# One load with a repeated source for the base blocks, and the evacuations of transposed keys and values on ScalarE

## What is computed

```python
k_beta = k * beta[..., None]
v_beta = v * beta[..., None]
L = jnp.where(strict, jnp.einsum('bhncd,bhnmd->bhncm', k_beta, k) * decay, 0.0)
T_mat = lax.linalg.triangular_solve(eye + L, jnp.broadcast_to(eye, L.shape),
                                    left_side=True, lower=True, unit_diagonal=True)
u = jnp.einsum('bhncm,bhnmd->bhncd', T_mat, v_beta)
w = jnp.einsum('bhncm,bhnmd->bhncd', T_mat, k_beta * jnp.exp(g)[..., None])
k_to_end = k * jnp.exp(g_last[..., None] - g)[..., None]
```

## Time and profile before

| | us |
|---|---|
| median of 3 runs | 1362.94 (1361.47 to 1365.14) |
| profiled execution, whole | 1355.06 |
| its span, first to last instruction | 1353.3 |
| PE busy | 1294.6 (96%) |
| PE weight loads busy | 1088.4 (80%) |
| DVE busy | 940.7 (70%) |
| ACT busy | 708.2 (52%) |
| POOL busy | 228.8 (17%) |
| mean granted PE clock | 0.977 of full speed |

### The profile page before, as it was taken

The page is one execution under the profiler, slowest core; times in us unless marked ns, Lnnn a source line. Parts: engine busy times, 40 slices in busy tenths (PEclk is TensorE's granted clock), DMA queues, the critical chain, the costliest instruction groups (busy, mean ns, idle before and its releaser), DMA issues.

```text
span 1353.3 us, 20838 instructions
## 1 busy us (share of the span) xinstructions
PE 1294.6 (96%) x6906; PEld 1088.4 (80%) x6906; DVE 940.7 (70%) x1703; ACT 708.2 (52%) x1288; POOL 228.8 (17%) x293
## 2 busy tenths in 40 slices
PE   5999979999999979989999999999999999999996
PEld 4676769857888757878888888888888888888885
DVE  5697696646765535566978888888788885555554
ACT  5454444424434664546566656665666555444442
POOL 5321120122201130000222322232222220000000
PEclk9899989979999988999999999999999999999999
DMA  8352543313633403553555455554555556555551
GB/s 329 124 204 108 139 175 119 131 63 123 199 116 127 167 19 125 191 183 124 191 201 197 178 194 187 186 190 182 206 176 202 179 199 221 197 202 188 187 186 62
DMA packets 32695, 225.85 MB, mean 167 GB/s; under 512 B 4352, under 2 KB 4736, under 8 KB 5888
## 3 DMA queue, kind: packets, MB, share of 16 engines
q1 hardware_dynamic: 30528, 218.12, 45.2%
q10 hardware_dynamic: 2112, 7.00, 2.1%
HBM read 222.87 MB, written 2.23 MB: 166 GB/s over the span
## 4 chain that ended last, share of the span: by engine, by line
PE 87%; DVE 8%; ACT 2%; issue 1%; DMA 1%; ACTq 1%; POOL 0%; DVEq 0%; SPq 0%; POOLq 0%
PE bank L1219 35%; PE bank L1221 17%; PE bank L1508 8%; PE bank L1510 8%; PE bank L1509 8%; DVE w_lo L752 3%; ACT w_hi L409 1%; DVE arena L777 1%; PE bank L1302 1%; PE bank L1255 1%; PE bank L1373 1%; PE bank L1313 1%; PE bank L1273 1%; DVE ssum L822 1%; DMA raw<-in_wts 1%
## 5 line engine op out<-in xcount | busy, mean ns | idle before, releaser
L1219 PE MATMUL bank<-xhl,w_hi 128*128 128x512 f32 x2304 | 826.6, 403 | 21.3 <-DVE w_lo L752 15.9
L752 DVE TENSOR_TENSOR w_lo<-raw,w_hi 128x512 fp32r<-128x512 f32 x816 | 574.9, 727 | 250.2 <-ACT w_hi L409 248.0
L409 ACT ACTIVATE w_hi<-raw 128x512 fp32r<-128x512 f32 x816 | 500.4, 628 | 392.2 <-PE bank L1221 233.8
L1221 PE MATMUL bank<-xhl,w_lo 128*128 128x256 f32 x2304 | 645.7, 280 | 0.0
L1219 PEld LDWEIGHTS bank<-xhl,w_hi 128*128 128x128 f32 x2304 | 437.3, 190 | 140.3 <-issue 20.8
L1221 PEld LDWEIGHTS bank<-xhl,w_lo 128*128 128x128 f32 x2304 | 438.8, 190 | 0.1
L1508 PE MATMUL bank<-w_hi,ffn_act 128*128 128x512 f32 x352 | 136.9, 389 | 0.0
L1510 PE MATMUL bank<-w_hi,ffn_act 128*128 128x512 f32 x352 | 136.9, 389 | 0.0
L1509 PE MATMUL bank<-w_lo,ffn_act 128*128 128x512 f32 x352 | 136.9, 389 | 0.0
L381 POOL TENSOR_TENSOR arena<-arena,token_scale 128x256 f32<-128x256 f32 x88 | 79.4, 918 | 308.8 <-DVE arena L757 186.4
L1141 DVE SCALAR_TENSOR_TENSOR arena<-arena,fcw 128x256 f32<-128x256 f32 x176 | 85.3, 485 | 23.9 <-DVE arena L1141 1.5
(11 more groups left out here) (230 smaller groups left out, 847.1 us busy)
## 6 DMA issues: line engine op xcount, KB each, us to landing
raw<-in_wts SPq DMA_DIRECT2D x204, 1024.0 KB, 4.7
xfeat<-in_x SPq DMA_DIRECT2D x4, 512.0 KB, 9.5
xfeat<-in_x_tok ACTq DMA_DIRECT2D x1, 2048.0 KB, 7.8
arena<-base_rows ACTq DMA_DIRECT2D x16, 128.0 KB, 5.0
out_y<-xfeat SPq DMA_DIRECT2D x4, 512.0 KB, 2.9
arena<-in_post_gains ACTq DMA_DIRECT2D x1, 1024.0 KB, 4.7
down_gain<-in_post_gains ACTq DMA_DIRECT2D x1, 1024.0 KB, 4.7
arena<-in_w_ba ACTq DMA_DIRECT2D x1, 320.0 KB
```

Source lines behind the costliest of these rows:

```text
L409: nc.scalar.activation(w_hi[:, i % RING, :], raw[:, slot, quarter * PIECE:(quarter + 1) * PIECE], ACT.Copy).then_inc(hi_ready, 1)
L752: V.tensor_tensor(w_lo[:, i % RING, :], raw[:, slot, quarter * PIECE:(quarter + 1) * PIECE], w_hi[:, i % RING, :].bitcast(f32), ALU.subtra ...
L1219: M(ps[j][:, :], w_hi[:, r % RING, w], xhl[:, k, :, :].rearrange("p a t -> p (a t)"), start=(k == 0), stop=False, skip_group_check=True)
L1221: last = M(ps[j][:, 0:T], w_lo[:, r % RING, w], xhl[:, k, 0, :], start=False, stop=(k == KT - 1), skip_group_check=True)
```

## The change

Two edits in ACT's and DVE's programs.

1. The eight loads of the packed base blocks become one, over all 128 partitions; its source names each block's 8 KB 16 times. It signals 16 instead of 128. Before ACT waits for the store to land, `follow(PLACE["pack", b] + 4)` is put in: ACT makes the pieces of places `pack`+2 to `pack`+4 between the store and the wait.
2. `head_tokens` moves from DVE to ACT: the four multiplications of each head become activations with the function Copy and a column as scale. On ACT head h-1's set stands after the exponentials of head h, at its old place; the last head's set stands before the store.

```diff
+                def head_tokens(h):
+
+                    follow(PLACE["tok", h])
+                    act_e.wait_ge(s("tok_mm"), h + 1)
+                    tp = ps[6 + h % 2]
+                    for j in range(NJ):
+                        nc.scalar.activation(proj[:, 16 + h, j * P:(j + 1) * P], tp[:, j * P:(j + 1) * P], ACT.Copy,
+                                             scale=cols[:, 2 + j, h:h + 1])
+                    nc.scalar.activation(proj[:, 8 + h, 0:P], tp[:, T:T + P], ACT.Copy, scale=cols[:, 5, h:h + 1])
+                    nc.scalar.activation(proj[:, 8 + h, P:T], tp[:, T + P:2 * T], ACT.Copy, scale=cols[:, 4, h:h + 1]
+                                         ).then_inc(s("tok_sb"), 1)
+
+                act_e.wait_ge(s("cols_sb"), 1)
                 for h in heads:
 
                     follow(PLACE["bc", h])
                     act_e.wait_ge(s("ddiff"), h + 1)
                     nc.scalar.activation(dm[:, h % 2, :], dm[:, h % 2, :], ACT.Exp).then_inc(s("dexp"), 1)
                     nc.scalar.activation(eg(h), ps[4 + h % 2][:, T + P:2 * T], ACT.Exp).then_inc(s("eg_ready"), 1)
+                    if h > BH * b:
+                        head_tokens(h - 1)
+                head_tokens(BH * b + BH - 1)
 
                 follow(PLACE["pack", b] + 1)
                 act_e.wait_ge(s("packed"), b + 1)
                 act_e.dma_start(scratch[b], packed.rearrange("p u i -> p (u i)")).then_inc(s("scratch_in"), 16)
+                follow(PLACE["pack", b] + 4)
                 act_e.wait_ge(s("scratch_in"), 16 * (b + 1))
-                for n_ in range(NBLK):
-                    act_e.dma_start(
-                        block_l[BASE * n_:BASE * (n_ + 1)].rearrange("p j u i -> p (j u i)"),
-                        scratch[b][BASE * n_:BASE * (n_ + 1), :].rearrange("(a j) n -> a (j n)", a=1).to_broadcast(
-                            [BASE, BASE * UNITS * BASE])).then_inc(s("block_in"), 16)
+                act_e.dma_start(block_l.rearrange("p j u i -> p (j u i)"),
+                                scratch[b].rearrange("(n j) (o x) -> n o (j x)", j=BASE, o=1).to_broadcast(
+                                    [NBLK, BASE, BASE * UNITS * BASE])).then_inc(s("block_in"), 16)
...
-                def head_tokens(h):
-
-                    follow(PLACE["tok", h])
-                    dve.wait_ge(s("tok_mm"), h + 1)
-                    tp = ps[6 + h % 2]
-                    for j in range(NJ):
-                        V.tensor_scalar(proj[:, 16 + h, j * P:(j + 1) * P], tp[:, j * P:(j + 1) * P],
-                                        cols[:, 2 + j, h:h + 1], None, ALU.mult)
-                    V.tensor_scalar(proj[:, 8 + h, 0:P], tp[:, T:T + P], cols[:, 5, h:h + 1], None, ALU.mult)
-                    V.tensor_scalar(proj[:, 8 + h, P:T], tp[:, T + P:2 * T], cols[:, 4, h:h + 1], None, ALU.mult
-                                    ).then_inc(s("tok_sb"), 1)
...
-                    if t_:
-                        head_tokens(h - 1)
-                    if t_ < BH:
                         head_products(h)
...
                     if i == 1:
-                        dve.wait_ge(s("block_in"), 16 * NBLK * (batch + 1))
+                        dve.wait_ge(s("block_in"), 16 * (batch + 1))
```

## The result

| | before | changed |
|---|---|---|
| median, 20 runs each | 1361.88 us | 1374.68 us |
| lowest to highest | 1344.3 to 1365.5 | 1355.94 to 1377.34 |
| profiled execution, its span | 1355.06, 1353.3 | 1375.01, 1373.3 |

The changed kernel is slower. The ratio is 1.0087, with a 95% interval of 1.006 to 1.0114, and a second series gave 1.0117 (1.0072 to 1.0161). I had forecast 1359.6 us and the range ended at 1364.5: wrong, on the side of rival (2).

A forecast was written before the change was run, and what follows sets the result against it. PE (87% of the chain) bounds the kernel, so only its waits count: 3.3 us from batch 0's loads, 0 from batch 1 and evacuations, subtracted from the median 1362.94, gave 1359.6 us; range 1356 to 1364.5.

The forecast's parts named there:

- rival (2): Single load: repeated source keeps 1.03 us packets, on eight engines; lands after 16.5 us, 13 to 14 us slower, 1376; chance 0.12.
- ACT's stall: ACT at the store's wait and block loads: the 5.3 us stall goes, and ACT is level with PE by 165.
- The gain with the load out of the way: Batch 0's base solve: first row at 168.9 instead of 172.18, so spread and gain 3.3 us earlier.
- 25.1 us of DVE work: DVE from the base solve's first row to the spread in batch 0: no idle time, same length after the change.
- Batch 1: Second DeltaNet batch: late start paid back before the end; gain 0 to 0.2 us, taken as 0.
- rival (3): PE's clock holds in batch 0's shorter transposes gap: 1.4 us more, gain 4.7, 1358.2; chance 0.21, shared with larger DVE gains.
- The landing: Single load, needed 8.9 to 9.4 us after issue: hidden at 164.2 (0.45), or late by 1 to 3.5 us (0.22).
- rival (1): Single load on half the engines: 5.1 us, hidden or landing at 169.3; 0.4 us at most; fast form has no own chance.
- The cover: PE during DVE's wait for the load: rival (2) counted no PE stop between the late first row and the transposes.
- ring of pieces: Weight pieces made ahead for PE: the ring holds 8, so PE doesn't feel a stall at once.
- The evacuations: Head multiplications on ACT: 0.35 us each, 1.1 a set, PE's last wait 1.2; cost -0.3 to +0.3 a batch, taken at 0.

The follow-up runs named there:

- second series: The whole change run once more, unaltered, beside the kernel before on the same chip: 1367.68 us, ratio 1.0117.
- 128 different rows: Whole change, but the single load brings 128 different 8 KB rows of the weights instead of eight blocks repeated 16 times: 1357.28 us, ratio 0.9954.
- different rows in eight groups: Whole change, but the single load takes eight groups of 16 rows from the weights, nothing repeated, outermost dimension 8: 1369.4 us, ratio 1.0079.
- light weights: Whole change, but each later load of weights brings only 64 of 2048 columns: 1348.87 us in a single execution.
- first group: Four kernels on one chip beside before: loads alone 1.0064, 128 different rows 0.9954, different rows in eight groups 1.0079, 16 outermost 0.997.

## Why the prediction was wrong

**ACT's stall: right.** Three pieces at once, the load issued at 159.35, ACT level with PE by place 79.

**The gain with the load out of the way: right.** 3.3 us worked out, 3.75 measured with 128 different rows (198.01 - 194.26). That the 25.1 us of DVE work stay and that PE still waits 3.8 us held too. Batch 1 gained nothing, as forecast: its wait was 1.0 to 1.1 us wherever the load was fast. The clock didn't hold in the shorter gap, against rival (3): with 128 different rows the granted clock was 0.53 from 194 to 196 us, and from the first transposes (L1354 there) to the first product of the inverse it took 5.4 us (194.26 to 199.66), as before, not 3.9.

**The landing: wrong, and this is the step that failed.** The forecast took the fast packet time for granted and named the load's half of the engines as harmless, 5.1 us at 0.32 us a packet. The mechanism of rival (1) was right and two of its terms were mis-sized. A packet took 0.62 us, not 0.32, so 9.9 us. And the weights added 5 us, not 2.6: I let one chunk meet the load, but SP issues a chunk every 5.6 us, so a load that takes 15 us shares its engines with almost three. In the profile of the changed kernel a load of weights took 12.2 us in this stretch, against 4.7. Together 17 us, and with them the loss I had put at rival (2)'s door. Rival (2)'s cause, a repeated source that makes packets slow, was wrong: different rows in eight groups were as slow. That its 1376 us lie near the 1374.68 measured is luck: its first term, a first row 5.9 us late, was 4.3 in the trace, and part of the measured loss comes from elsewhere (below).

The rule of the Trainium skill (DMA: Bandwidth & Descriptors, Why a DMA increments its semaphore by 16 and not by 1) agrees with the runs on the number of engines: about 16 packets at once for 128 and for 16 outermost, 8 for 8 and 4 for 4, as counted above. The landings go the same way: 128 outermost 4.8 us, 16 outermost 7.0 to 7.3 (10.3 to 11.6 in batch 1), 8 outermost 16 to 18 (12 with light weights), 4 outermost 25 to 27. Why 16 outermost is slower than 128 on as many engines, that rule doesn't say. Another rule of the Trainium skill, on ports (SBUF — State Buffer, Door 1: The DMA port swizzle), would explain why a packet takes about twice the time, if each engine fills neighbouring partitions in order; no run here took that apart.

**The cover: missed in batch 0, without a price there.** Rival (2) has no stop of PE between the late first row and the transposes, as if the ring of pieces carried PE over it. In batch 0 PE stopped after four pieces, since the addition that empties its next bank is queued behind the first row on DVE. That is the 4.8 us, and they moved no start behind them, as shown above. In batch 1 all four additions stand ahead of the first row, and the ring did carry PE: DVE's wait of 8.6 us gave it one of 0.2.

**The evacuations: right in the waits, open in the time.** 0.37 us and more each against 0.35, a wait of 1.2 us for the last set, no new wait. Whether they cost something in the time of whole executions stays open: alone 1.0024 (0.999 to 1.0058), and with the fast load 0.997 with them and 0.9987 and 0.9977 without, all within their intervals.

**Batch 1: wrong by the same landing.** First row at 367.89, 12.9 us later than before. Of these 6.3 were there when the blocks were stored (348.06 against 341.81); the other 6.7 are to be held against the 7.5 of rival (2). The transposes wait 3.9 us instead of 1.0.

**What the time is made of.** The profiled executions differ by 20 us, the medians by 12.8. 3.7 us are shown at the transposes of batch 0, and 0.9 behind them, since from L1356 to L1255 it took 6.2 us (201.74 to 207.96) instead of 5.3. 2.9 are shown in the wait of batch 1. With PE idle there its clock falls in batch 1 too, which it didn't before:

```profile
384.00:388.00 4.00, 1.87 (x7) 1.77 (x8) 3.97 (x8) 0.71 (x2) 1.71 (x2) 0.53 0.09 39
388.00:392.00 4.00, 4.00 (x17) 3.51 (x17) 1.77 (x4) 1.52 (x3) 0.00 (x0) 0.62 0.48 135
```

(columns as in the earlier trace rows: the granted clock is 0.53, then 0.62.) From L1356 to L1255 it now takes 392.31 - 386.13 = 6.2 us instead of 3.9: 2.3 more. That makes 9.8 us that the two traces tie to the load. The loads alone cost 6.9 us by their medians and 8.7 by their ratio (1.0064 of 1360.17). The remaining 3 us of the whole change I can't place. One trace hints that the evacuations on ACT have a part in it: with them on DVE the load of batch 0 landed in 15.8 us and not in 17.1 to 17.3, and the transposes started 2.0 us earlier. In batch 1 the landings were alike, so this isn't shown.

## What to carry to other kernels

The shape of the source decided how many DMA engines carried a transfer. When several small loads are joined into one, look at the outermost dimension of both sides; here 8 in the source gave eight engines, 16 and 128 gave sixteen. Storing the data twice to get to 16 turned 17 us into 7 in batch 0 and 18 into 10 to 12 in batch 1, which took the loss away. And before counting on a cover, look for the first thing queued behind the late wait on the same engine: here it was a bank's addition, and it cut the cover from seven pieces to four. A transfer that meets a steady stream must be sized against all of the stream that passes while it lasts.

## What the runs showed of the hardware

Two things move the time by several microseconds between executions, whatever the kernel. In the first group before ran from 1342.25 to 1367.05 us.

The first is the pace of PE at full clock. Matmuls in 700 to 900 us, of the changed kernel and of the same kernel in its second series:

```profile
700.00:900.00 200.00, 200.00 (x1133) 173.52 (x1133) 163.79 (x301) 120.76 (x223) 50.36 (x52) 1.00 0.53 188
```

```profile
700.00:900.00 200.00, 200.00 (x1155) 174.93 (x1154) 166.58 (x307) 121.31 (x225) 51.95 (x55) 1.00 0.53 188
```

2% between two executions of the same code, at a granted clock of 1.00 and with PE busy all the time. There were two paces: four of the thirteen profiles, before's among them, had 1155 or 1156 matmuls in this stretch, the other nine 1133 or 1134. From the first transposes of L1550 to the end of the span it took 745.2 us in before and in the second series, and 753.2 in the first profile of the changed kernel. That is 8 of the 20 us between the two profiles: at L1550 the changed kernel was 12.0 us behind (620.12 and 608.09), at the end 20. The second series' profile has the waits of the first and a span of 1355.9 us. What sets the pace isn't shown.

The second is how long PE's clock stays at half (1.2 in place of 2.4 GHz) at the start of batch 1, in before and in the kernel with 16 outermost and the evacuations on DVE:

```profile
280.00:320.00 40.00, 36.64 (x143) 24.50 (x141) 16.42 (x33) 12.56 (x21) 4.61 (x6) 0.79 0.18 57
```

```profile
280.00:320.00 40.00, 37.13 (x181) 26.72 (x182) 22.67 (x52) 16.01 (x31) 8.72 (x14) 0.96 0.21 74
```

The mean granted clock of these 40 us was 0.79 and 0.96, and between 0.74 and 0.96 in all the profiles, with the same wait of 2.7 us ahead of it in before and in the changed kernel. What ends it isn't settled. For a change of a few microseconds, the start of a named instruction ahead of both (L1356 of batch 0: 201.74 and 201.86 in the two profiles of the changed kernel, 194.40 and 194.08 in those of the other) told more than whole executions did.
